# Product-key rankings at one step a slot, and a gather ring of ten rows from slot 80 on

## The chip, the cores and the metric

One NeuronCore of a Trainium2 chip runs one kernel launch. The metric is device time in microseconds. The engines are TensorE (PE; PEld is its weight load), VectorE (DVE), ScalarE (ACT), GpSimd (POOL, which here only issues gathers) and SyncE (SP, which issues plain loads). All are in order and meet by semaphores.

## What is computed

A decoder trunk of two layers over 256 tokens of width 1024, in float32. Layer 0 mixes tokens by differential attention, layer 1 by a gated short convolution. Behind each mixer stands an expert layer (PEER): 8 heads, and for each head the 16 best of 128 x 128 experts by product keys.

```python
q = (xt @ w_q).reshape(T, PEER_HEADS, 2, PEER_HALF)
s = jnp.einsum('thpd,hpkd->thpk', q, sub_keys)
s_top, i_top = lax.top_k(s, PEER_TOPK)
cand = s_top[:, :, 0, :, None] + s_top[:, :, 1, None, :]       # 16 x 16 sums a head
best, pos = lax.top_k(cand.reshape(T, PEER_HEADS, -1), PEER_TOPK)
idx = jnp.take_along_axis(cand_idx, pos, axis=-1)
gates = jax.nn.softmax(best, axis=-1)
# for a token c and its 8 x 16 experts:
act = jnp.einsum('chkd,cd->chk', u_tab[ib], xb)
act = jax.nn.gelu(act) * gb
out = jnp.einsum('chk,chkd->cd', act, v_tab[ib])
```

Every token reads 128 rows of u and 128 of v in each layer, rows of 1024 float32 each: that is most of what the kernel moves.

## The kernel before, in words

The 256 tokens are two blocks of 128 (one token a partition), and with the two layers there are four windows n = 0 to 3: layer n // 2, block n % 2. A window has 128 slots, one for each of a token's 128 experts; the main loop runs over 512 slots. In a slot

- POOL gathers 128 rows of 2048 float32 (u and v of one expert for each token, 1 MB) into one row of `ring` (L620). `ring` has RING = 8 rows. Gather s may start when the matmuls of slot s - 8 are done (`v_used`), and the head's `idx` must be there (`idx_ready`, once in 16 slots).
- DVE waits for the landing and makes the dot product of the u half with `xf` (L1215, `dot`).
- ACT makes gelu, weight and `diag`, the weight on a diagonal of 128 x 128 (L829, L831, L835, `weigh`).
- PE multiplies `diag` with the v half into `acc` (L555, `add_expert`), two slots behind, and counts up `v_used`.

All other work of a window is done beside the slots of the window before it. Each piece is a generator ("side") that yields the slot at which its next step is due, and `along` runs what is due behind each slot's own work, on each engine's own loop. The due slots stand in `AT`, relative to slot (n - 1) x 128, so window n's entries lie in the slots of window n - 1 (and run over into its own). For window 0, which the straight code in `front` prepares, some chunks come late: LATE_RANK_PROJECT for heads 2 to 7, LATE_IN_PROJECT for the attention input of block 1.

The pieces that matter here: `x` turns h of the new layer into xT, `in0` to `in5` are the mixer's input projections, `out0`, `out1` its output, `f` turns h again, `wq0` to `wq3` are the four query projections for experts (two heads each). A projection is 8 steps at 8 slots (`project`, L318). 13 slots behind its start DVE begins `ranked` (L1013 and on): a generator of 16 steps with 15 yields between them: MAX8, FIND_INDEX8, MATCH_REPLACE8 and again for the scores, the candidate sums, the same for the candidates, then one-hot product and sum for the index, and `idx_ready`. `paced(steps, at, per_slot)` spreads them, so far two a slot; ACT's exponential of the gates (`exponential_gates`) follows at step 8 and DVE's `gate_values` at 9. `finish` adds `acc` to h one slot into the next window, and PE waits for that (`acc_read`) before it overwrites `acc`; `scale_for_mixer` follows for the windows that have a successor to prepare.

SP loads weights (2 MB each) in a fixed order into the two places of `wring`, each when its former content was used. `vrows` (V of attention, 8 KB a partition) and `bias` (8 KB) are used by windows 0 and 1 alone. `rows1` holds query rows and some mixer rows. PSUM banks alternate in the pools pp, tt, ss, ff, in the order in which PE takes them.

Of the kernel before, what the change touches and what calls it, by code (L numbers as in the profile page):

```python
# [11 lines left out]
ACT = mybir.ActivationFunctionType  # L12
AX = mybir.AxisListType

P = 128
D = 1024
# [12 lines left out]
RING = 8  # L29
WINDOWS = DEPTH * (SEQ // P)  # L30
# [26 lines left out]
def steady_of(n):  # L57
# [11 lines left out]
         wq0=94, wq1=104, wq2=114, wq3=124),  # L69
    dict(x=3, in2=8, in4=16, in3=24, in5=32, in0=40, in1=48, z0=26, z1=42, turn_z0=27, turn_z1=43, turn_g0=49, turn_g1=57,  # L70
         conv0=30, conv1=46, times=59, out0=62, out1=70, h0=71, f0=72, h1=79, f1=80, scale=80,
         wq0=84, wq1=94, wq2=104, wq3=114),
# [3 lines left out]
LATE_RANK_PROJECT = {1: 0, 2: 25, 3: 41}  # L76
LATE_IN_PROJECT = {2: 9, 1: 17, 3: 33}

# [34 lines left out]
def build(nc, consts, x_rows, x_cols, bias_rows, ffn_rows, w_qkv, w_o, conv_w_in, conv_w_out, peer_w_q, peer_keys, peer_uv, out):  # L113
    with ExitStack() as ctx:
# [30 lines left out]
        vrows = sb("vrows", [P, 2, D])  # L145
        bias = sb("bias", [P, HEADS, SEQ])
        kT = sb("kT", [P, HEADS * SEQ + 16])
        qTa = sb("qTa", [P, HEADS, P])
        yT = qTa
        scratch = sb("scratch", [P, 2 * D])  # L150
# [34 lines left out]
        dots = sb("dots", [P, RING])  # L185
        gelu = sb("gelu", [P, RING])
        weight = sb("weight", [P, RING])
# [40 lines left out]
        uv_in = [sem(f"uv_in{i}") for i in range(RING)]  # L228
# [29 lines left out]
        def ring_at(s):  # L258
            return (s + 4) % RING

        def slot(s):

            return ring[:, ring_at(s), :], uv_in[ring_at(s)], 16 * (s // RING + 1)
# [35 lines left out]
        def _(pe):  # L299
# [222 lines left out]
            def gated_input(n):  # L522
# [4 lines left out]
                for i, c in enumerate((2, 4, 3, 5, 0, 1)):  # L527
# [3 lines left out]
                    yield from project(pp, n, "in", c, xT, at[f"in{c}"])  # L531
# [69 lines left out]
        def _(pool):  # L601
            for n in range(WINDOWS):
                for k in range(SLOTS):
# [3 lines left out]
                    if s < RING:  # L607
                        if ring_at(s) < 2:
                            written(pool, ff, (1, "in", 4))
                        elif ring_at(s) < 4:  # L610
                            written(pool, ff, (1, "in", 5))
                        elif ring_at(s) < 6:
# [11 lines left out]
        def _(act):  # L624
# [76 lines left out]
            def front():  # L701
# [28 lines left out]
                copy_y(0, 1)  # L730
                copy_f(0, 0)
# [12 lines left out]
            def rank(n, c, at, rank_at):  # L744
# [6 lines left out]
                yield rank_at + 8  # L751
# [50 lines left out]
            def gated_input(n):  # L802
                at = steady_of(n)
                for c in range(2):
                    yield at["x"] + c + 1
                    if c == 0:
                        written(act, pp, (n - 1, "wq", 3))
                    first = n // 2 * KT + 4 * c
                    copy_scaled((n, "x", c), xT[:, 4 * c:4 * c + 4, :], gain_mix[:, first:first + 4])
# [14 lines left out]
            def weigh(s):  # L824

                r = s % RING
                at = s % (2 * SLOTS)
                act.wait_ge(dot_done, s + 1)
                nc.scalar.activation(gelu[:, r:r + 1], dots[:, r:r + 1], ACT.Gelu_apprx_tanh).then_inc(gelu_done, 1)  # L829
# [446 lines left out]
```

## Time and profile before

| | us |
|---|---|
| three runs: median (lowest to highest) | 1601.99 (1601.55 to 1603.75) |
| the profiled execution | 1602.38 |
| its span | 1600.5 |
| PE busy | 1362.0 (85%) |
| DVE busy | 1012.6 (63%) |
| ACT busy | 593.4 (37%) |
| POOL busy | 559.7 (35%) |

The span runs from the first instruction to the last. The page of the profile cuts it into 40 slices of 40 us; for each it gives every engine's busy share in tenths and what the DMA engines moved in GB/s. A GB/s figure below its neighbours is transfer time lost. The list of waits says which engine waited for what, in total; the chain of waits goes back from the end by what released each step. Slots can be told in the trace by counting the dot products (L1215): slot 0 begins at 109.7 us, slot 128 at 498.2, slot 256 at 888.9, slot 384 at 1274.7.

### The profile page before, as it was taken

Reading aid. Unit: us, or ns where it says so; the run is one execution under the profiler, and the core shown is the slowest. Engines: PE = TensorE matmul, PEld = TensorE weight load, DVE = VectorE, ACT = ScalarE, POOL = GpSimd, SP = SyncE. Lnnn points to the kernel's source line nnn. Section 1 sums busy time; section 2 is a strip of 40 time slices with the busy share of each in tenths; the row PEclk is TensorE's granted clock in tenths of the full one; section 3 lists DMA queues with packets and bytes.
Section 4 is the critical chain, followed back from the end, with each engine's and each line's share of the span. In section 5 each row is a group of like instructions: output and inputs, shape, how many; then the busy total and the mean of one; then the engine's idle time right before and its main releaser. Section 6 shows DMA issues by size and latency. Waiting matters only on the chain.

```text
span 1600.5 us, 12987 instructions
## 1 busy us (share of the span) xinstructions
PE 1362.0 (85%) x3288; PEld 583.8 (36%) x3288; DVE 1012.6 (63%) x2442; ACT 593.4 (37%) x1809; POOL 559.7 (35%) x516
## 2 busy tenths in 40 slices
PE   7899899797987998897987799979888778777776
PEld 3454344343433343333433343434343332222222
DVE  4576879855498854445598854444568875444444
ACT  1324354533334442333334442333334443333333
POOL 0023333343333343352433343433333344333331
PEclk9999999899999999999999899999999999999999
DMA  9469999999999999999999899999999999999997
GB/s 399 197 245 422 422 413 414 368 395 421 422 425 414 400 424 421 422 422 422 422 422 422 349 398 423 422 422 422 422 425 418 351 347 423 421 421 422 421 422 321
DMA packets 82440, 639.67 MB, mean 400 GB/s; under 512 B 9152, under 2 KB 9280, under 8 KB 10560
## 3 DMA queue, kind: packets, MB, share of 16 engines
q0 software_dynamic: 73728, 536.90, 81.6%
q1 hardware_dynamic: 7344, 95.95, 14.3%
q10 hardware_dynamic: 1296, 6.00, 0.9%
q8 instruction: 28, 0.46, 0.1%
q14 instruction: 44, 0.36, 0.1%
HBM read 637.77 MB, written 1.05 MB: 399 GB/s over the span
## 4 chain that ended last, share of the span: by engine, by line
DMA 32%; DVE 29%; PE 29%; ACT 6%; issue 4%; DVEq 0%; POOL 0%; SPq 0%; POOLq 0%; ACTq 0%
DMA ring<-in_peer_uv_dram,idx 31%; PE acc L555 17%; DVE ring L1215 12%; PE pp L318 8%; DVE top_i L1001 2%; DVE pos L1001 2%; DVE top L997 1%; PE acc L318 1%; ACT L829 1%; DVE pick L1043 1%; DVE best L997 1%; DVE row_f L1046 1%; DVE pick L1040 1%; ACT weight L831 1%; ACT L699 1%
## 5 line engine op out<-in xcount | busy, mean ns | idle before, releaser
L555 PE MATMUL acc<-ring,diag 128*128 128x512 f32 x2048 | 1002.7, 617 | 169.4 <-ACT diag L835 155.7
L1215 DVE CUSTOM_DVE_ANT_0 ring<-ring,xf 128x1024 f32<-128x1024 f32 x512 | 624.8, 1226 | 486.9 <-DMA ring<-in_peer_uv_dram,idx 475.7
L620 POOL DMA_INDIRECT ring<-in_peer_uv_dram,idx x512 | 559.5, 1093 | 1017.2 <-PE acc L555 889.9
L555 PEld LDWEIGHTS acc<-ring,diag 128*128 128x128 f32 x2048 | 380.7, 195 | 720.9 <-issue 704.0
L829 ACT ACTIVATE gelu<-dots 128x1 f32<-128x1 f32 x512 | 103.5, 202 | 859.9 <-DVE dots L1215 859.5
L318 PE MATMUL pp<-wring,xT 128*128 128x512 f32 (+1 forms) x496 | 247.7, 590 | 1.2 <-ACT xT L639 1.2
L835 ACT ACTIVATE diag<-const,weight 128x128 f32<-128x128 f32 x512 | 205.4, 401 | 16.7
L831 ACT ACTIVATE weight<-gelu,gates 128x1 f32<-128x1 f32 x512 | 150.8, 295 | 16.6
L318 PEld LDWEIGHTS pp<-wring,xT 128*128 128x128 f32 x496 | 94.8, 194 | 109.9 <-issue 107.0
L318 PE MATMUL pp<-wring,qTa 128*128 128x512 f32 x112 | 57.2, 599 | 0.0
L331 PE MATMUL tt<-const,rows 128*128 128x128 f32 x144 | 23.8, 291 | 22.4 <-ACT rows L633 12.0
L1215 DVE DVE_READ_ACCUMULATOR2_ANT dots<- 128x1 f32 x512 | 42.3, 83 | 0.0
L390 PE MATMUL ss<-keysT,qT 128*128 128x128 f32 x128 | 20.7, 311 | 23.2 <-issue 23.2
L997 DVE MAX8 top<-score 128x8 f32<-128x128 f32 x128 | 28.1, 281 | 10.0 <-ACT score L695 9.3
L331 PEld LDWEIGHTS tt<-const,rows 128*128 128x128 f32 x144 | 17.4, 146 | 46.2 <-ACT rows L633 23.2
L1001 DVE FIND_INDEX8 top_i<-top,score 128x8 uint32<-128x128 f32 x128 | 34.2, 285 | 0.0
L318 PEld LDWEIGHTS pp<-wring,qTa 128*128 128x128 f32 x112 | 21.5, 193 | 26.8 <-issue 26.8
L390 PEld LDWEIGHTS ss<-keysT,qT 128*128 128x128 f32 x128 | 18.4, 217 | 35.2 <-issue 35.2
L1001 DVE FIND_INDEX8 pos<-best,pick 128x8 uint32<-128x256 f32 x64 | 26.1, 419 | 0.0
L318 PE MATMUL pp<-wring,xf 128*128 128x512 f32 x48 | 24.9, 601 | 0.0
L997 DVE MAX8 best<-pick 128x8 f32<-128x256 f32 x64 | 24.2, 417 | 0.6
L829 ACT ACT_TABLE_LOAD x19 | 24.4, 1283 | 0.3
(109 smaller groups left out, 570.2 us busy)
## 6 DMA issues: line engine op xcount, KB each, us to landing
wring<-in_peer_w_q_dram SPq DMA_DIRECT2D x16, 2048.0 KB, 11.7
wring<-in_conv_w_in_dram SPq DMA_DIRECT2D x12, 2048.0 KB, 11.7
wring<-in_w_qkv_dram SPq DMA_DIRECT2D x5, 2048.0 KB, 12.3
ring<-in_peer_uv_dram,idx POOLq DMA_INDIRECT x512, 15.3
wring<-in_conv_w_out_dram SPq DMA_DIRECT2D x4, 2048.0 KB, 11.8
ring<-in_w_qkv_dram SPq DMA_DIRECT2D x3, 2048.0 KB, 32.1
wring<-in_w_o_dram SPq DMA_DIRECT2D x3, 2048.0 KB, 12.7
ring<-in_w_qkv_dram SPq DMA_DIRECT2D x2, 1024.0 KB, 8.7
```

The lines of the kernel that those rows point to most:

```text
L318: mm = nc.tensor.matmul(bank[:, 0:width], src[:, k, :], by_row[:, k, columns], start=(k == 0), stop=(k == KT - 1))
L331: t = nc.tensor.transpose(bank[:, j * P:(j + 1) * P], tile, ident)
L390: mm = nc.tensor.matmul(bank[:, j * P:(j + 1) * P], qT[:, j, :], keysT[:, 4 * c + j, :], start=True, stop=True)
L555: mm = nc.tensor.matmul(acc[half][:, :], diag[:, s % RING, :], row[:, D + half * 512:D + (half + 1) * 512], start=(k == 0), stop=(k == SLO ...
L620: nc.gpsimd.indirect_dma_start(dst, None, uv_dram, bass.IndirectOffsetOnAxis(idx[:, at:at + 1], 0)).then_inc(landed, 16)
L699: nc.scalar.activation(best_e[:, js[0]:js[-1] + 1, :], best_e[:, js[0]:js[-1] + 1, :], ACT.Exp).then_inc(best_exp, len(js))
L829: nc.scalar.activation(gelu[:, r:r + 1], dots[:, r:r + 1], ACT.Gelu_apprx_tanh).then_inc(gelu_done, 1)
L831: nc.scalar.activation(weight[:, r:r + 1], gelu[:, r:r + 1], ACT.Copy, scale=gates[:, at:at + 1]).then_inc(weight_ready, 1)
L835: nc.scalar.activation(diag[:, r, :], ident, ACT.Copy, scale=weight[:, r:r + 1]).then_inc(diag_ready, 1)
L997: ins = nc.vector.max(t, v)
L1001: ins = nc.vector.max_index(i, t, v)
L1215: nc.vector.tensor_tensor_reduce(row[:, 0:D], row[:, 0:D], xf[:, s // SLOTS % 2, :], 1.0, 0.0, ALU.mult, ALU.add, dots[:, s % RING:s % RIN ...
```

## The change

`pieces(n, c)` gives the steps a slot of ranking (n, c): one, but two for the rankings (0,1), (0,2) and (1,0). The ACT and DVE steps for the gates move behind the longer ranking (`gates_from`). The wq projections get other due slots: 94, 104, 116, 128 for window 1, and 84, 98, 112, 126 for windows 2 and 3. Since the last one now overlaps `x` of the next window, `x` is turned into a tile of its own, `xTm`, the second half of `rows1`, and the queries take only the first half; ACT's waits follow.

`vrows` and `bias` become views of one tile, `spare`, 16 KB a partition, and from slot 80 on `spare` gives two more ring rows. Slots 80 and 81 are gathered into them once attention is done with bias and V (`logit_max` at 4, `values` (1,1) written); every later slot waits for the matmuls of ten slots before. `dots`, `gelu` and `weight` get 16 columns; `diag` stays at 8.

```diff
 RING = 8
+LONG_RING = 10
+LONG_FROM = 80
+SMALL = 16
...
-         wq0=94, wq1=104, wq2=114, wq3=124),
+         wq0=94, wq1=104, wq2=116, wq3=128),
...
-         wq0=84, wq1=94, wq2=104, wq3=114),
+         wq0=84, wq1=98, wq2=112, wq3=126),
...
+RANK_PIECES = {(0, 1): 2, (0, 2): 2, (0, 3): 1, (1, 0): 2}
...
+def pieces(n, c):
+
+    return RANK_PIECES.get((n, c), 1)
+
+
+def gates_from(n, c):
+
+    return 15 // pieces(n, c) + 1
...
-        vrows = sb("vrows", [P, 2, D])
-        bias = sb("bias", [P, HEADS, SEQ])
+        spare = sb("spare", [P, KT * CHUNK])
+        vrows = spare[:, 0:2 * D].rearrange("p (b d) -> p b d", b=2)
+        bias = spare[:, 2 * D:].rearrange("p (h k) -> p h k", h=HEADS)
...
+        xTm = rows1[:, D:2 * D].rearrange("p (k t) -> p k t", k=KT)
...
-        uv_in = [sem(f"uv_in{i}") for i in range(RING)]
+        uv_in = [sem(f"uv_in{i}") for i in range(LONG_RING)]
...
-        def ring_at(s):
-            return (s + 4) % RING
+        row_of = [(s + 4) % RING for s in range(RING)]
+        while len(row_of) < LONG_FROM:
+            row_of.append(row_of[-RING])
+        row_of += range(RING, LONG_RING)
+        while len(row_of) < ALL:
+            row_of.append(row_of[-LONG_RING])
+        row_uses = [row_of[:s].count(row_of[s]) for s in range(ALL)]
+        ring_rows = [ring[:, r, :] for r in range(RING)]
+        ring_rows += [spare[:, r * 2 * D:(r + 1) * 2 * D] for r in range(LONG_RING - RING)]
...
-            return ring[:, ring_at(s), :], uv_in[ring_at(s)], 16 * (s // RING + 1)
+            return ring_rows[row_of[s]], uv_in[row_of[s]], 16 * (row_uses[s] + 1)
...
-            return rows1[:, c * CHUNK:(c + 1) * CHUNK]
+            return rows1[:, c % 2 * CHUNK:(c % 2 + 1) * CHUNK]
...
-                    yield from project(pp, n, "in", c, xT, at[f"in{c}"])
+                    yield from project(pp, n, "in", c, xTm, at[f"in{c}"])
...
+                    elif s < LONG_FROM:
+                        pool.wait_ge(v_used, s - RING + 1)
+                    elif s < LONG_FROM + LONG_RING - RING:
+                        pool.wait_ge(logit_max, 4)
+                        written(pool, pp, (1, "values", 1))
                     else:
-                        pool.wait_ge(v_used, s - RING + 1)
+                        pool.wait_ge(v_used, s - LONG_RING + 1)
...
-                if n == 1 and c == 0:
-                    written(act, pp, (0, "wq", 3))
+                if n and c == 0:
+                    written(act, pp, (n - 1, "wq", 3))
...
+                written(act, pp, (0, "in", 5))
                 copy_f(0, 0)
...
-                yield rank_at + 8
+                yield rank_at + gates_from(n, c)
                 exponential_gates(n, c)
...
-                    if c == 0:
-                        written(act, pp, (n - 1, "wq", 3))
+                    if c == 0 and n == 3:
+                        written(act, pp, (2, "in", 1))
...
-                yield from paced(ranked(n, c), at, 2)
-                yield at + 9
+                yield from paced(ranked(n, c), at, pieces(n, c))
+                yield at + gates_from(n, c) + 1
                 gate_values(n, c)
```

## Rows read from the trace of the kernel before

**Rows 1.** The page: busy time; DMA share (tenths) and GB/s by slice.

```profile
PE 1362.0 (85%) x3288; PEld 583.8 (36%) x3288; DVE 1012.6 (63%) x2442; ACT 593.4 (37%) x1809; POOL 559.7 (35%) x516
...
DMA  9469999999999999999999899999999999999997
GB/s 399 197 245 422 422 413 414 368 395 421 422 425 414 400 424 421 422 422 422 422 422 422 349 398 423 422 422 422 422 425 418 351 347 423 421 421 422 421 422 321
DMA packets 82440, 639.67 MB, mean 400 GB/s; under 512 B 9152, under 2 KB 9280, under 8 KB 10560
```

**Rows 2.** List of waits, whole span: total us, times, longest.

```profile
POOL ring L620 <- PE acc L555: 889.9, 480, 8.8
...
DVE ring L1215 <- DMA ring<-in_peer_uv_dram,idx: 475.7, 316, 6.3
...
DVE best_s L1065 <- ACT best_e L699: 19.0, 16, 1.4
...
PE acc L555 <- DVEq L1209: 12.8, 3, 4.9
```

**Rows 3.** Stretches: busy us of PE, PEld, DVE, ACT, POOL; clock, DMA, GB/s.

```profile
220.00:260.00 40.00, 40.00 (x124) 19.85 (x122) 31.88 (x96) 12.34 (x36) 14.06 (x15) 1.00 1.00 404
280.00:340.00 60.00, 48.20 (x122) 21.56 (x121) 48.73 (x133) 30.86 (x91) 25.28 (x23) 0.91 0.94 367
480.00:540.00 60.00, 49.42 (x130) 22.42 (x129) 52.29 (x162) 26.69 (x74) 20.24 (x18) 0.94 0.99 402
600.00:860.00 260.00, 225.59 (x534) 98.58 (x533) 149.54 (x339) 91.66 (x285) 96.75 (x85) 0.96 1.01 422
880.00:960.00 80.00, 68.79 (x156) 29.89 (x155) 54.16 (x137) 34.08 (x101) 30.18 (x26) 0.91 0.94 374
960.00:1240.00 280.00, 245.83 (x583) 106.52 (x582) 157.79 (x338) 97.51 (x303) 100.79 (x93) 0.96 1.01 422
1240.00:1320.00 80.00, 61.46 (x139) 25.11 (x138) 66.80 (x185) 34.21 (x100) 32.69 (x29) 0.96 0.91 350
1320.00:1580.00 260.00, 204.92 (x422) 71.53 (x421) 128.28 (x209) 93.42 (x312) 103.86 (x105) 1.00 1.01 421
```

**Rows 4.** Chain of waits inside the plateau: start us, us, what.

```profile
1369.83 1.23 DVE ring L1215
...
1372.21 1.97 PE acc L555 x4
...
1374.44 15.25 DMA ring<-in_peer_uv_dram,idx
...
1389.71 1.23 DVE ring L1215
```

**Rows 5.** Gathers (L620) issued in 1240:1320 us, time from issue to landing.

```profile
DMA to landing us min/median/max: 5.2/7.8/12.5
```

**Rows 6.** Dots back to back: ns min/median/max, first and last start us.

```profile
L1215 DVE CUSTOM_DVE_ANT_0 ring<-ring,xf x6: 1221/1223/1225, 1303.6 to 1309.3; 128x1024 f32<-128x1024 f32 x6
```

**Rows 7.** Dot products during the ranking of slots 353 to 361.

```profile
L1215 DVE CUSTOM_DVE_ANT_0 ring<-ring,xf x9: 1224/1224/1226, 1178.3 to 1203.8; 128x1024 f32<-128x1024 f32 x9
```

**Rows 8.** Dot products over the next cycle of ten slots.

```profile
L1215 DVE CUSTOM_DVE_ANT_0 ring<-ring,xf x11: 1222/1226/1227, 1208.2 to 1239.4; 128x1024 f32<-128x1024 f32 x11
```

**Rows 9.** DVE by line and form in 1178.3:1205.4: busy us, mean ns, idle before.

```profile
L1043 DVE TENSOR_TENSOR pick<-pick,top_f 128x1024 f32<-128x1024 f32 x1 | 1.2, 1224 | 0.0
```

**Rows 10.** Timeline of DVE at slots 257 and 259: start us, us, what.

```profile
893.23 1.51 DVE L1207 TENSOR_TENSOR h<-h,acc 128x512 f32<-128x512 f32 x2
...
902.94 1.23 DVE L875 CUSTOM_DVE_ANT_0 scratch<-h 128x1024 f32<-128x1024 f32 x1
...
906.45 1.23 DVE L1215 CUSTOM_DVE_ANT_0 ring<-ring,xf 128x1024 f32<-128x1024 f32 x1 [0.19 <-DVE scale_mix L871]
```

**Rows 11.** By line, whole span: busy us, mean ns of one, idle before.

```profile
L318 PE MATMUL pp<-wring,xT 128*128 128x512 f32 (+1 forms) x496 | 247.7, 590 | 1.2 <-ACT xT L639 1.2
```

**Rows 12.** Weight loads (L583, SP), whole span, time from issue to landing.

```profile
DMA to landing us min/median/max: 7.8/11.8/25.5
```

More of the change, by code:

```diff
@@ L184, in build @@
         gains = sb("gains", [P, 2])
-        dots = sb("dots", [P, RING])
-        gelu = sb("gelu", [P, RING])
-        weight = sb("weight", [P, RING])
+        dots = sb("dots", [P, SMALL])
+        gelu = sb("gelu", [P, SMALL])
+        weight = sb("weight", [P, SMALL])
         diag = sb("diag", [P, RING, P])
@@ L607, in _ @@
                     if s < RING:
-                        if ring_at(s) < 2:
+                        if row_of[s] < 2:
                             written(pool, ff, (1, "in", 4))
-                        elif ring_at(s) < 4:
+                        elif row_of[s] < 4:
                             written(pool, ff, (1, "in", 5))
-                        elif ring_at(s) < 6:
+                        elif row_of[s] < 6:
                             written(pool, ff, (1, "in", 0))
@@ L805, in gated_input @@
                     yield at["x"] + c + 1
-                    if c == 0:
-                        written(act, pp, (n - 1, "wq", 3))
+                    if c == 0 and n == 3:
+                        written(act, pp, (2, "in", 1))
                     first = n // 2 * KT + 4 * c
-                    copy_scaled((n, "x", c), xT[:, 4 * c:4 * c + 4, :], gain_mix[:, first:first + 4])
+                    copy_scaled((n, "x", c), xTm[:, 4 * c:4 * c + 4, :], gain_mix[:, first:first + 4])
                 for c in (2, 4, 3, 5, 0, 1):
@@ L824, in weigh @@
             def weigh(s):
-                r = s % RING
+                r, m = s % RING, s % SMALL
                 at = s % (2 * SLOTS)
                 act.wait_ge(dot_done, s + 1)
-                nc.scalar.activation(gelu[:, r:r + 1], dots[:, r:r + 1], ACT.Gelu_apprx_tanh).then_inc(gelu_done, 1)
+                nc.scalar.activation(gelu[:, m:m + 1], dots[:, m:m + 1], ACT.Gelu_apprx_tanh).then_inc(gelu_done, 1)
                 act.wait_ge(gelu_done, s + 1)
-                nc.scalar.activation(weight[:, r:r + 1], gelu[:, r:r + 1], ACT.Copy, scale=gates[:, at:at + 1]).then_inc(weight_ready, 1)
+                nc.scalar.activation(weight[:, m:m + 1], gelu[:, m:m + 1], ACT.Copy, scale=gates[:, at:at + 1]).then_inc(weight_ready, 1)
                 act.wait_ge(weight_ready, s + 1)
@@ L834, in weigh @@
                     act.wait_ge(v_used, s - RING + 1)
-                nc.scalar.activation(diag[:, r, :], ident, ACT.Copy, scale=weight[:, r:r + 1]).then_inc(diag_ready, 1)
+                nc.scalar.activation(diag[:, r, :], ident, ACT.Copy, scale=weight[:, m:m + 1]).then_inc(diag_ready, 1)
             front()
@@ L1124, in late @@
                 yield at
-                yield from paced(ranked(0, c), at, 2)
-                yield at + 9
+                yield from paced(ranked(0, c), at, pieces(0, c))
+                yield at + gates_from(0, c) + 1
                 gate_values(0, c)
@@ L1158, in experts @@
                 yield at
-                yield from paced(ranked(n, c), at, 2)
-                yield at + 9
+                yield from paced(ranked(n, c), at, pieces(n, c))
+                yield at + gates_from(n, c) + 1
                 gate_values(n, c)
@@ L1215, in dot @@
                 nc.vector.tensor_tensor_reduce(row[:, 0:D], row[:, 0:D], xf[:, s // SLOTS % 2, :], 1.0, 0.0, ALU.mult, ALU.add,
-                                               dots[:, s % RING:s % RING + 1]).then_inc(dot_done, 1)
+                                               dots[:, s % SMALL:s % SMALL + 1]).then_inc(dot_done, 1)
             front()
```

## The prediction

> **What bounds the kernel now.** I began with the page [rows 1]. No engine is full: PE is busy for 85% of the span, DVE for 63%. The DMA line stands at 9 almost everywhere, and the GB/s line has a plateau at 421 to 425 with dents. Then the list of waits [rows 2]: POOL, which issues the gathers, waits 889.9 us for PE to release ring rows (acc), and DVE waits 475.7 us for gathers to land. So the gathers are a closed loop of 8 ring rows, and the transfer itself sets the pace where the loop is full. The table by stretch says where it is not [rows 3]: 422, 422 and 421 GB/s in the three long stretches, but 404, 367, 402, 374 and 350 GB/s in five short ones. At 422 GB/s as the full rate, the transfer time lost in a dent is its length times (422 minus rate)/422: 1.7 us in 220:260, 7.8 in 280:340, 2.8 in 480:540, 9.1 in 880:960 and 13.6 in 1240:1320. Together 35.0 us. What is left of the span is 639.67 MB at 422 GB/s (1516 us), the start before the gathers, and the drain behind the last one, none of which the change touches.
>
> What makes the dents? In all five DVE is busy for most of the time, 66.8 of 80 us in the last [rows 3]. The loop's own time in the plateau is in the chain of waits [rows 4]: from one dot product to the one eight slots later 19.88 us (2.485 a slot), of which 15.25 us is the gather from its issue on and 4.6 us dot, gelu, weight, diag, matmul and release. A gather with an empty queue before it lands in 5.2 us [rows 5]. So DVE may lag behind the landings by about 15.25 - 5.2 = 10 us before the queue runs dry. Where DVE is the bound, dots with nothing between them follow each other in (1309.3 - 1303.6)/5 = 1.14 us [rows 6], so 2.485 - 1.14 = 1.35 us a slot is free for side work. During a ranking 8 slots take 1203.8 - 1178.3 = 25.5 us [rows 7]: 25.5 - 8 x 1.14 = 16.4 us of ranking in 16 steps, two a slot, 2.05 us where 1.35 are free. Each ranking therefore adds 0.7 x 8 = 5.6 us of lag. With its gate step the cycle is 10 slots in 1239.4 - 1208.2 = 31.2 us against 24.9 us of transfers [rows 8], 6.3 us of lag each. Four of them in a row, less 5 us for a weight load (2.10 MB at 422 GB/s), give about 20 us of lag and lost transfer before slot 393: past the 10 us, and the dent is explained.
>
> **The change, part by part.**
> Rankings one step a slot. The same instructions, 16.4 us, over 16 slots: 1.02 us a step on average, and the largest single step is 1.22 us [rows 9]. All are under 1.35 us, so such a ranking adds no lag. The wq projections of windows 2 and 3 move to 84, 98, 112, 126, so a cycle is 14 slots: 34.8 us of transfer time against 14 x 1.14 + 16.4 + 0.6 (gates) = 33.0 us. The 1.4 us that DVE waits at worst for ACT's exponential [rows 2] arises when dots are back to back and fades when it waits for landings anyway; at its worst 34.4, still under 34.8.
> Stage around 384: four cycles over some 60 slots, 149 us of transfers. DVE: 68.4 of dots, 65.6 of rankings, 2.4 of gates, 1.5 for adding acc to h [rows 10]: 137.9. No lag beyond 4 us, so the 13.6 us go; I take 13.3.
> Around 256: the same plus the mixer's scale, 902.94 to 906.45 = 3.5 us [rows 10]: 141.4 against 149. Burst at slots 257 to 259: 5 us over two slots, lag 5 to 7 us. Of 9.1 us I take 8.8.
> Around 128: ranking (1,0) keeps two steps a slot, and (1,2) now begins at 129 while (1,1) runs to 132. Slots 129 to 132 hold 8 steps (8.2), a gate step (0.6) and 5.0 of adding and scale: 13.8 against 5.4 free, 8.4 us of lag on top of some 2. That is over the limit of 8 rows with its PE wait below and under that of ten. Of 2.8 us I take 2.6.
> Around slots 54 to 70 (280:340) only ranking (0,3) is spread; attention's steps stay, and eight rows stay. The bounds are 0 and 7.8 us; the ranking's 5.6 us of lag are the larger part of what fills the slack, so I take 5.0. 220:260 has ranking (0,2) as before: 0.
>
> A ring of ten from slot 80. Two more gathers in flight add 2 x 2.485 = 5.0 us of slack: 15 us. In the plateau this is worth nothing: the transfers are back to back and a gather only waits longer in the queue. It covers the bursts at 128 and 256, and the wait of PE for acc_read (12.8 us in three, the longest 4.9) [rows 2], which puts off the release of two rows. Slots 80 and 81 wait for logit_max and values (1,1), which PE issues at slot 64, while POOL comes to slot 80 after v_used 72: nothing waits. Behind them on POOL's in-order queue slot 82 waits for v_used 73 only. A slot now issues ten ahead, so slot 128 wants its idx when v_used is 119, against a ranking done at 115; 240 against 246 at the next boundary; later heads have 15 slots or more to spare. Cost 0.
>
> The moved projections. Each is 8 slots of two PE records of 0.5 us [rows 11] beside the 1.97 us of a slot's own matmuls [rows 4]: 23.8 us against 8 x 2.485 + 5.0 = 24.9 us with its weight load. The counts are unchanged and the wq ones lie further apart. ACT's copies and SP's loads keep their order: queries, turned and scores move with their chunk. The load of (n+1,in,4) waits for (n,wq,3) to be written, now at slot 133 or 135, and is wanted at 144: at least 8 slots, 20 us, against a median load of 11.8 us [rows 12]. Hidden; if the cover were gone it would be 11.8 us three times at most. x in its own tile (xTm) takes away ACT's wait for (n-1,wq,3) that would now bite; the waits added on (0,in,5) and (2,in,1) are for matmuls long done; dots, gelu, weight of 16 columns: 0.
>
> Sum: 13.3 + 8.8 + 2.6 + 5.0 = 29.7 us, and 1602.4 - 29.7 = 1572.7 in terms of the profiled execution (span 1600.5 plus 1.9 around it), which is 0.4 us above the median of the runs. I say 1572.5.
>
> A rule against it stands beside this sum. Rows 1 show 400 GB/s on average and rows 3 422. The Trainium skill (DMA: Bandwidth & Descriptors, Specifications) gives the HBM limit of a core as about 358 GB/s. By that the stream would be bound by HBM and the kernel would need some 1787 us for its bytes; the trace is faster than that, so the measurement decides.
>
> **Rivals.**
> B, only the deeper ring counts (8%): the lag comes not from the steps' density but from what holds PE at a boundary, its wait for acc_read. For it: PE's wait is real [rows 2]. Against it: the lag is there by slot 383 before any boundary work. It gives at most 5.0 us at each boundary: 2.8 + 5 + 5 = 12.8, hence 1589.6.
> C, the plateau rises (4%): deeper queue, higher rate. The rows' best stretch is 422 and the page's best slice 425 [rows 1, 3]: 0.7% of some 1200 us is 8 us more, 1564. Against it: the rate is 421 to 422 whether a gather spends 8 or 15 us in the queue. The Trainium skill (same page, Where 436 GB/s comes from) puts the fabric's ceiling at 435 GB/s; by that it could be an estimated 36 us, about 1537. No row comes near it.
> D, it does not do what it says (4%): rankings overlap, the lag is only moved, and the dents deepen at 128 as they vanish elsewhere: 1602.
> E, slower (4%): weight loads. Ten gathers queued ahead make each load later; PE waits in order, and behind the waiting projection stand all add_expert calls, hence v_used and every gather. The place is the eight tight loads a window (spacing 8 slots, 24.9 us with the load's own time). If a load took 30 us, 18 loads x 5.1 = 92 us, about 1665; it outweighs the gain from 26.6 us a load on. For it: the longest load in the trace took 25.5 us [rows 12]. Against: the median is 11.8 us beside eight queued gathers, and in proportion to ten that is 14.8.
>
> **How the numbers follow.** Forecast A: 80%, 1572.5, its own range 1565 to 1585: below, all 35.0 us and a little of C; above, nothing from 280:340 (5 us) and 2 to 3 us left in each boundary. The range of 8 in 10 is that one; B, D and E lie above it, C at its lower edge. About 0.2% (3 us) is what a measurement can tell from no change. Faster 0.92 (A, B, C), within 0.2% 0.04 (D), slower 0.04 (E).
>
> **What would show it.** In the profile after: GB/s at 421 or 422 in the slices of slots 256 and 384, no slice of the second half under 415 but the last; DVE's wait for landings spread over the rankings, where before it waited for none; gathers from slot 82 on landing about 5 us later after their issue in the plateau (20 us for 15.3); dots during rankings 2.5 us apart. A dent left at 280:340 of 2 to 3 us. The forecast is wrong if the dents stay with DVE idle in them (B), if PE waits for wring (E), or if DVE is still busy without a pause through slots 353 to 400 (D).

## The result, and the profile after

The changed kernel takes 1580.78 us (median of 4 runs, 1580.00 to 1582.67) beside 1601.77 us for the kernel before on the same chip: a ratio of 0.9872, 95% interval 0.9857 to 0.9887. It is faster by 21 us. The forecast was 1572.5, within 1565 to 1585: sign and mechanism were right, and of 29.7 us some 21 came. The profiled execution of after took 1580.29 us, its span 1578.5, 22.0 less than before.

The page of after, the lines that answer to [rows 1]:

```profile
PE 1358.9 (86%) x3288; PEld 588.6 (37%) x3288; DVE 1005.5 (64%) x2442; ACT 594.9 (38%) x1809; POOL 574.2 (36%) x516
...
DMA  9469999999999999999999999999999999999995
GB/s 399 206 245 422 422 409 409 406 422 422 422 422 421 423 423 421 423 423 421 422 422 421 407 424 422 423 422 421 423 421 422 421 407 421 421 421 422 421 422 241
DMA packets 82441, 639.68 MB, mean 405 GB/s; under 512 B 9152, under 2 KB 9280, under 8 KB 10560
```

The same engines do the same instructions. The dents of 347 to 400 GB/s of [rows 1] are shallow now (406 to 409), but the last slice is lower: 241 for 321.

The same five dents and three quiet stretches, by stretch, to set beside [rows 3] (columns as there; the last stretch ends at 1540 because the last gather now lands at 1570.1):

```profile
220.00:260.00 40.00, 39.57 (x122) 19.44 (x120) 32.57 (x98) 12.40 (x37) 14.61 (x14) 1.00 1.00 396
280.00:340.00 60.00, 50.26 (x129) 23.13 (x128) 51.30 (x138) 33.24 (x100) 30.63 (x25) 0.91 1.00 411
480.00:540.00 60.00, 50.90 (x128) 23.06 (x127) 51.22 (x149) 23.68 (x72) 20.72 (x18) 0.91 1.01 421
600.00:860.00 260.00, 224.43 (x529) 98.57 (x527) 143.46 (x315) 91.26 (x289) 100.39 (x89) 0.95 1.01 422
880.00:960.00 80.00, 74.31 (x179) 33.61 (x180) 62.01 (x164) 32.15 (x96) 29.97 (x26) 0.93 1.01 415
960.00:1240.00 280.00, 245.85 (x578) 107.93 (x577) 156.67 (x340) 101.38 (x318) 110.01 (x96) 0.95 1.01 422
1240.00:1320.00 80.00, 67.78 (x155) 27.25 (x154) 71.21 (x194) 35.58 (x103) 34.89 (x32) 0.98 1.01 414
1320.00:1540.00 220.00, 171.42 (x352) 59.40 (x350) 108.75 (x179) 81.79 (x267) 86.89 (x89) 1.00 1.01 421
```

What each dent lacks of 422 GB/s, by the forecast's formula: 2.5, 1.6, 0.1, 1.3 and 1.5 us, together 7.0 where before had 35.0. So 28 us of transfer time were closed, against 29.7 forecast. Yet the last gather landed only 22.0 us earlier, and 1.6 of them were there at the first gather, before anything differs. The missing part shows in the end of the stream, in stretches of 20 us. First after:

```profile
1520.00:1540.00 20.00, 15.64 (x32) 5.42 (x32) 9.87 (x16) 7.31 (x25) 7.55 (x9) 1.00 1.01 422
1540.00:1560.00 20.00, 15.63 (x32) 5.42 (x32) 9.87 (x16) 7.24 (x25) 4.62 (x5) 1.00 0.98 407
1560.00:1580.00 20.00, 11.73 (x24) 4.06 (x24) 7.54 (x12) 4.49 (x15) 0.00 (x0) 0.91 0.12 48
```

and the kernel before:

```profile
1560.00:1580.00 20.00, 15.75 (x34) 5.54 (x33) 9.31 (x17) 7.18 (x24) 6.55 (x7) 1.00 1.01 420
1580.00:1600.00 20.00, 12.56 (x26) 4.07 (x25) 8.43 (x14) 5.39 (x18) 0.00 (x0) 1.00 0.56 231
```

Before, the last gather landed at 1592.0 us; 231 x 20/422 = 10.9 us of transfers lie in the last 12.0 us, 1.1 us are lost. After, it landed at 1570.1; (407 + 48) x 20/422 = 21.6 us of transfers lie in the last 30.1, so 8.5 us are lost. (In both, 0.52 MB of output behind the last gather are counted, 1.2 us; the difference, 7.4 us, is the same without them.) PE still does 24 matmuls in the last stretch, four a slot, and the dots are still some 2.48 us apart, while next to nothing moves: 48 GB/s. Gathers complete one after another out of bytes that were nearly all moved before.

Why, the landing marks of the trace tell. Every gather leaves 16 marks on its row's semaphore. They are read here as one for each of the 16 DMA engines, made when its share is done; the trace doesn't name the engine, and the experiments below bear the reading out. The gather has landed with the last of the 16. From these marks (worked out from the trace's semaphore records: us from the first to the last of the 16, and in brackets from the last but one to the last):

```
slot    before      after        ring of 8   two steps a slot
128    3.3 (1.2)   2.6 (0.2)    2.7 (0.1)    3.3 (0.4)
272    0.5 (0.1)   6.7 (3.6)    2.1 (1.2)    4.3 (3.8)
392    1.8 (1.4)  11.8 (4.7)    5.5 (2.5)    3.7 (3.4)
511    2.7 (0.9)  10.8 (4.9)    6.6 (2.9)    2.6 (0.1)
```

The 16 engines drift apart. In after, at the end, 15 of them are at least 4.9 us ahead of the last one. Averaged over the 16 marks, the lead over the last one is 9.1 us at slot 511, and 1.7 us before: 7.4 us more, which is just what the drain lost more. Before, each dent let the slow ones catch up while the fast ones stood idle (0.5 us between first and last at slot 272, 1.8 at 392), and a mean over 16 engines counts that idling as loss even where the slowest engine doesn't pause. That is theory S below: the pace is that of the slowest DMA engine, so closing a dent gives only what the slowest engine idled. Its rival M: transfer time is what the mean rate says, and the rest was lost elsewhere.

### The profile page after: what moved, and what is told of

Its sections match the earlier page's. It is cut to its first block, busy times and chain, and to the rows that moved or that the text cites. A ratio compares the mean times of both kernels' runs of the same rounds, so it can differ in the third digit from the quotient of the medians.

```text
span 1578.5 us, 13059 instructions
## 1 busy us (share of the span) xinstructions
PE 1358.9 (86%) x3288; PEld 588.6 (37%) x3288; DVE 1005.5 (64%) x2442; ACT 594.9 (38%) x1809; POOL 574.2 (36%) x516
## 3 DMA queue, kind: packets, MB, share of 16 engines
q1 hardware_dynamic: 7344, 95.95, 14.5%
## 4 chain that ended last, share of the span: by engine, by line
DMA 43%; PE 32%; DVE 16%; issue 4%; ACT 4%; DVEq 0%; POOL 0%; SPq 0%; POOLq 0%; ACTq 0%
DMA ring<-in_peer_uv_dram,idx 24%; PE acc L578 19%; DMA spare<-in_peer_uv_dram,idx 18%; PE pp L341 9%; DVE ring L1244 5%; DVE spare L1244 1%; PE acc L341 1%; PE tt L354 1%; DVE top_i L1030 1%; ACT diag L864 1%; DVE row_f L1075 1%; DVE top L1026 1%; ACT weight L860 1%; DVE pick L1072 1%; DVE pick L1069 1%
## 5 line engine op out<-in xcount | busy, mean ns | idle before, releaser
L578 PE MATMUL acc<-ring,diag 128*128 128x512 f32 x1696 | 831.4, 619 | 126.9 <-ACT diag L864 117.1
L648 POOL DMA_INDIRECT ring<-in_peer_uv_dram,idx x424 | 476.9, 1125 | 832.2 <-PE acc L578 707.5
L1244 DVE CUSTOM_DVE_ANT_0 ring<-ring,xf 128x1024 f32<-128x1024 f32 x424 | 518.7, 1226 | 397.6 <-DMA ring<-in_peer_uv_dram,idx 387.4
L578 PEld LDWEIGHTS acc<-ring,diag 128*128 128x128 f32 x1696 | 318.1, 196 | 575.4 <-issue 562.7
L578 PE MATMUL acc<-spare,diag 128*128 128x512 f32 x352 | 172.9, 618 | 28.8 <-ACT diag L864 28.7
L1244 DVE CUSTOM_DVE_ANT_0 spare<-spare,xf 128x1024 f32<-128x1024 f32 x88 | 107.8, 1225 | 96.6 <-DMA spare<-in_peer_uv_dram,idx 95.2
L341 PE MATMUL pp<-wring,xT 128*128 128x512 f32 (+1 forms) x304 | 148.6, 585 | 1.2 <-ACT xT L667 1.2
L648 POOL DMA_INDIRECT spare<-in_peer_uv_dram,idx x88 | 97.1, 1104 | 144.1 <-PE acc L578 141.7
L578 PEld LDWEIGHTS acc<-spare,diag 128*128 128x128 f32 x352 | 65.2, 196 | 124.0 <-issue 123.8
L341 PE MATMUL pp<-wring,rows 128*128 128x512 f32 x192 | 98.8, 596 | 0.0
## 6 DMA issues: line engine op xcount, KB each, us to landing
wring<-in_peer_w_q_dram SPq DMA_DIRECT2D x16, 2048.0 KB, 11.9
wring<-in_conv_w_in_dram SPq DMA_DIRECT2D x12, 2048.0 KB, 11.9
wring<-in_conv_w_out_dram SPq DMA_DIRECT2D x4, 2048.0 KB, 11.9
```

The source lines that it names most:

```text
L341: mm = nc.tensor.matmul(bank[:, 0:width], src[:, k, :], by_row[:, k, columns], start=(k == 0), stop=(k == KT - 1))
L578: mm = nc.tensor.matmul(acc[half][:, :], diag[:, s % RING, :], row[:, D + half * 512:D + (half + 1) * 512], start=(k == 0), stop=(k == SLO ...
L648: nc.gpsimd.indirect_dma_start(dst, None, uv_dram, bass.IndirectOffsetOnAxis(idx[:, at:at + 1], 0)).then_inc(landed, 16)
L1244: nc.vector.tensor_tensor_reduce(row[:, 0:D], row[:, 0:D], xf[:, s // SLOTS % 2, :], 1.0, 0.0, ALU.mult, ALU.add, dots[:, s % SMALL:s % SM ...
```

## The experiments

The diffs are against the changed kernel, with cuts marked by dots. Ratios are to the kernel before, run beside each experiment.

**Which half of the change does it?** The ring of ten is taken back, the spread rankings stay:

```diff
-LONG_RING = 10
+LONG_RING = 8
```

> The changed kernel with a ring of eight throughout (LONG_RING = 8): the spread rankings alone. Theory S (the density of the rankings made the dents, and what is left is set by the slowest of the 16 DMA engines): most of the gain stays, about 1583 to 1588, with some us lost where adding acc to h and the mixer's scale meet a ranking at slots 128 and 256. Rival B (only the two extra rows count): the dents are back at 880:960 and 1240:1320 and the time is 1595 or more. If the two parts share the gain evenly: about 1590.

Measured: 1581.04 us (1580.53 to 1582.33), ratio 0.9861 (0.9844 to 0.9877). That is less than all three expectations, and it can't be told from the whole change (0.9872; a repetition of the changed kernel gave 1580.37, 0.9856, 0.9838 to 0.9875). By stretch:

```profile
480.00:540.00 60.00, 50.04 (x124) 22.63 (x123) 49.38 (x143) 23.54 (x70) 18.77 (x17) 0.91 0.99 399
...
880.00:960.00 80.00, 73.20 (x178) 33.05 (x179) 61.94 (x166) 31.52 (x96) 27.27 (x26) 0.93 1.00 410
...
1240.00:1320.00 80.00, 67.79 (x155) 27.27 (x154) 70.95 (x190) 35.22 (x102) 35.55 (x32) 0.98 1.01 410
```

Its dents at 480:540 (399), 880:960 and 1240:1320 are deeper than those of after (421, 415, 414): 3.1, 0.9 and 0.8 us more by the mean rate, and yet the end isn't later. The engines' spread at the end is 6.6 us for 10.8. Under M after should have been 5 us faster; under S the two rows only let fast engines run further ahead. Their mean lead at slot 511 is 5.2 us here and 9.1 in after.

The other half alone: the ring of ten, with all rankings at two steps a slot at their old slots:

```diff
-         wq0=94, wq1=104, wq2=116, wq3=128),
+         wq0=94, wq1=104, wq2=114, wq3=124),
...
-         wq0=84, wq1=98, wq2=112, wq3=126),
+         wq0=84, wq1=94, wq2=104, wq3=114),
...
-RANK_PIECES = {(0, 1): 2, (0, 2): 2, (0, 3): 1, (1, 0): 2}
+RANK_PIECES = {}
...
-    return RANK_PIECES.get((n, c), 1)
+    return RANK_PIECES.get((n, c), 2)
```

> The changed kernel with all rankings at two steps a slot and the old due slots of the query projections: the ring of ten alone. Theory S: the 7 us at slots 64 to 80 are lost again (eight rows there), the lag of slots 353 to 393 still exceeds the slack by some 5 us, so 1590 to 1594. Rival B: 1580 to 1584, since the ring alone covers the lag.

Measured: 1592.77 us, ratio 0.9934 (0.9917 to 0.9950), 10.7 us faster than before.

```profile
280.00:340.00 60.00, 48.29 (x122) 21.73 (x121) 48.98 (x133) 30.88 (x91) 27.19 (x24) 0.91 0.95 365
480.00:540.00 60.00, 49.96 (x129) 23.13 (x128) 52.22 (x162) 26.70 (x74) 19.68 (x18) 0.91 1.01 422
...
880.00:960.00 80.00, 67.02 (x150) 28.21 (x149) 56.48 (x140) 35.27 (x107) 32.36 (x27) 0.94 0.97 387
...
1240.00:1320.00 80.00, 60.76 (x139) 24.78 (x138) 67.17 (x178) 35.63 (x105) 36.65 (x29) 0.96 0.95 369
```

Ten rows add slack at three boundaries, as rival B had it: by the mean rate 2.8 + 2.5 + 3.6 = 8.9 us. Here deep dents remain, the engines are level at the end (spread 2.6 us), and the credit is full. The halves are not additive: alone they give 22 and 11 us, together 21 to 22. What the ring covers, the spread rankings no longer need.

A ring of nine (LONG_RING = 9), between the two:

> The changed kernel with a ring of nine from slot 80. Theory S: the fast DMA engines run ahead one gather less, which costs nothing while the slowest one always has work: within 2 us of 1580.8. If each row of the ring buys 2.5 us at each of the stages that still drain it: 1583 to 1588. It is also the control of the run with the extra loads, which needs the freed memory.

Measured: 1581.49 us (1579.57 to 1581.62), ratio 0.9865 (0.9848 to 0.9881). Eight, nine and ten rows are one time; the spread at the end is 6.6, 8.9 and 10.8 us.

**Which stage gives how much?** Only ranking (0,3) spread, ring of eight, the rest as before (`RANK_PIECES = {(0, 3): 1}`, default 2, the old wq slots):

> Ring of eight, every ranking at two steps a slot and at the old due slots, but (0,3) spread over 16 slots. It should give what the stage at slots 64 to 80 gives by itself, 7 us: 1594 to 1596. If spreading works only where all rankings are spread: no gain.

Measured: 1595.9 us, ratio 0.9968 (0.9958 to 0.9978): 5.1 us, where the expectation counted 7, and 280:340 is at 410 GB/s for 367. The term for slots 54 to 70 stood at 5.0. (The 7 us were read from two traces and held the 1.6 us that after was ahead at slot 0.)

Only the four rankings of window 3, slots 353 to 400 (ring of eight, every other ranking at two steps a slot and at its old due slots):

```diff
...
-AT = AT + (AT[2],)
+AT = AT + (dict(AT[2], wq0=84, wq1=98, wq2=112, wq3=126),)
...
-RANK_PIECES = {(0, 1): 2, (0, 2): 2, (0, 3): 1, (1, 0): 2}
+RANK_PIECES = {(3, 0): 1, (3, 1): 1, (3, 2): 1, (3, 3): 1}
```

> Ring of eight, only the four rankings of window 3 spread (with their new due slots). The stage around slot 384 alone. Theory S: 9 us, as between slots 384 and 400 of the two traces, 1592 to 1594. By the mean rate, as forecast: 13 us, 1588 to 1590.

Measured: 1590.33 us, ratio 0.9933 (0.9916 to 0.9949), 10.7 us. Its trace:

```profile
1240.00:1320.00 80.00, 68.84 (x172) 29.13 (x171) 70.72 (x199) 36.94 (x106) 39.19 (x33) 1.00 1.01 421
```

The dent is closed entirely, 13.5 us by the mean rate (350 to 421), and 10.7 arrive: between the two expectations. At slot 272 this kernel's engines stood level (0.4 us, dents before it are intact); at its end they are 7.6 us apart. The mean lead at slot 511 is 5.0 us for 1.7 before, 3.3 more, about the 2.8 us that are missing. The interval of 2.6 us either way wouldn't tell S from M by the time alone; the run with load on a single engine, below, does.

**Is it PE's instruction packets that hold one engine back?** The page lists packets of kind instruction (q8: 28 of 16 KB, q14: 45 of 8 KB) on the same DMA engines. PE's are taken down by doing the upper half of acc in the first slot of each window only; this kernel leaves out the expert sum of columns 512 to 1023 but for that slot:

```diff
-                for half in range(2):
+                for half in range(2 if k == 0 else 1):
...
-                                          start=(k == 0), stop=(k == SLOTS - 1))
+                                          start=(k == 0), stop=(half == 1 or k == SLOTS - 1))
```

> The changed kernel without three quarters of nothing but PE's second matmul of a slot: the upper 512 columns of the expert sum are made from the first slot of each window alone, the rest is left out. Gathers, dots, loads and all waits stay. PE's instruction stream becomes shorter (some 1000 of its 6600 instructions and their weight loads go), and with it the 16 KB packets in which it is fetched, from 28 to about 20. Theory S (one DMA engine carries them, 1.07 us each, and it sets the pace): about 8 us less, 1572 to 1575. Rival M (the mean rate): 0.13 MB less is 0.3 us, so 1580 to 1581. The landings' spread at the end falls from 10.8 us to 5 or less by S.

Measured: 1579.66 us, ratio 0.9864 (0.9847 to 0.9880). The expectation of 1572 to 1575 fell. q8 went from 28 to 20 packets and PE's matmuls from 3288 to 2272, and the engines' spread at the end stayed (11.1 us for 10.8); the last engine is 7.2 us behind the last but one, for 4.9. PE's packets don't sit on the slow engine. A third of PE's matmuls are gone, and the time is that of the changed kernel. Two dents did close, from 396 and 411 GB/s:

```profile
220.00:260.00 40.00, 29.95 (x89) 14.09 (x87) 35.69 (x111) 14.55 (x40) 15.27 (x14) 0.93 1.01 422
280.00:340.00 60.00, 39.33 (x91) 16.87 (x92) 48.10 (x124) 30.01 (x93) 29.46 (x25) 0.81 1.01 421
```

By the mean rate that is 3.9 us, and the measured 1.1 us isn't told from nothing.

**Does load on a single engine cost time while the mean rate doesn't change?** To the ring of nine, SP adds 72 loads of one partition, 8 KB each (three behind every weight load of windows 2 and 3, each waiting for the one before it):

```diff
+                if n > 1:
+                    for _ in range(3):
+                        ...
+                        sp.dma_start(spare[0:1, 2 * D:4 * D], in_dram[1][0][0:1, 0:2 * D]).then_inc(extra_in, 16)
+                        extras += 1
```

> As the ring of nine, with 72 extra loads of one row of 8 KB, three behind each weight load of windows 2 and 3. Together 0.59 MB, which is 1.4 us at 422 GB/s if all 16 DMA engines share one pace. Theory S: one row goes through one DMA engine, 72 x 0.31 = 22 us of its time. If that is the engine that lags already, the kernel becomes some 22 us longer; if it is another one, that engine first uses up its lead of about 10 us and the kernel becomes about 10 us longer. Rival M (the mean rate bounds, the missing 8 us lie elsewhere): 1 to 2 us longer.

Measured: 1588.0 us (1585.81 to 1590.90), ratio 0.9907 (0.9887 to 0.9926), 6.5 us over the ring of nine that ran beside it. The added bytes are 0.59 MB, 1.4 us at 422 GB/s. The stretch that holds part of the extra loads, here and in the ring of nine:

```profile
960.00:1240.00 280.00, 240.69 (x550) 104.26 (x551) 152.23 (x329) 98.74 (x309) 95.32 (x91) 0.94 1.00 412
...
960.00:1240.00 280.00, 243.24 (x575) 105.48 (x574) 157.27 (x339) 100.50 (x317) 106.92 (x96) 0.96 1.01 422
```

412 GB/s for 422, with more bytes to move: the others wait for the one. 72 packets of 309 ns are 22.2 us on that engine; 6.5 came out, less than either of S's expectations (10 and 22). The other 15.7 us fell into time that this engine had to spare, by S; the trace can't show that, since it doesn't name the engine. M's 1 to 2 us are excluded. That SP sent its weight loads late isn't the cause: they land in 11.9 us for 11.8, and no row of waits has PE waiting for wring.

**A load cut for 15 engines.** If the slow engine could be spared, the others would set the pace. Seven weight loads were cut into 120 and 8 partitions:

```diff
+                    sp.dma_start(place[0:120, :], matrix[c][0:120, :]).then_inc(landed, 16)
+                    sp.dma_start(place[120:P, :], matrix[c][120:P, :]).then_inc(w_rest_in, 16)
```

> The changed kernel with seven of its 2 MB weight loads cut in two: 120 partitions, and 8 partitions. If a load of 120 partitions is spread over 15 of the 16 DMA engines and the rest over 8 of the 15, the sixteenth has 7 x 128 KB = 34 us less to move. Theory S, if that engine is the lagging one: 8 to 10 us less, 1571 to 1573, and the landings' spread goes to about 3 us. If the lagging one is among the 8 that take the rest: 3 to 4 us more, 1584 to 1585. If it is another: 1581. Rival M: 1581 in each case, since the bytes are the same.

Measured: 1646.56 us, ratio 1.0275 (1.0255 to 1.0296): 66 us slower than the changed kernel, 9.4 us for each cut load, and outside every expectation. The spread of the 16 marks jumps to 15 to 29 us around them. Queue q1 here, and in after:

```profile
q1 hardware_dynamic: 7393, 95.95, 15.8%
...
q1 hardware_dynamic: 7344, 95.95, 14.5%
```

The same 95.95 MB take 15.8% of the engines' time, though the span is longer, with 49 packets more. It settles nothing about S; why the cut costs so much was not followed up.

**Whose instruction packets are they, then?** In the quiet end of after, two landings come late by 1.0 us. The timeline of DVE there (start us, us, what, in brackets its idle time before):

```profile
1327.14 1.23 DVE L1244 CUSTOM_DVE_ANT_0 ring<-ring,xf 128x1024 f32<-128x1024 f32 x1 [1.13 <-DMA ring<-in_peer_uv_dram,idx]
...
1330.64 1.23 DVE L1244 CUSTOM_DVE_ANT_0 ring<-ring,xf 128x1024 f32<-128x1024 f32 x1 [2.27 <-DMA ring<-in_peer_uv_dram,idx]
...
1333.08 1.23 DVE L1244 CUSTOM_DVE_ANT_0 ring<-ring,xf 128x1024 f32<-128x1024 f32 x1 [1.21 <-DMA ring<-in_peer_uv_dram,idx]
```

From dot to dot 3.50 us, then 2.44 where 2.485 is the pace. The same stands at 1483.14, 61 slots later. Each time one 8 KB packet of queue q14 was taken just before (1329.1 and 1480.8 us), and the gather's packet beside it took 958 and 968 ns for the usual 312. Two more packets of q14, at 1395.3 and 1474.9, stand beside gather packets of 687 ns, and no landing is late there. In the 61 slots between the two late landings DVE has 121 instructions in the trace, two a slot, the reading of the accumulator among them. So theory S2: the slowest engine is the one that also fetches DVE's instructions, and each fetch costs it about 1 us. The test is to add instructions on an engine with time to spare: five tiny ones behind each of 213 quiet slots, on DVE:

```diff
+                if s in QUIET:
+                    for j in range(5):
+                        at = s % 12 * 5 + j
+                        nc.vector.memset(small[:, at:at + 1], 0.0)
```

> The changed kernel with five tiny DVE memsets behind each dot of 213 slots in which DVE has no side work. DVE's time for them (at most 0.6 us a slot) lies in its wait for the landing. Theory S2 (the lagging DMA engine is the one that fetches DVE's instructions, 8 KB or some 128 instructions a time, about 1 us of delay each): 1065 instructions are 8.3 fetches, 8 us longer than the changed kernel, 1588 to 1590. Rival M (the mean rate of the 16 engines bounds): 0.07 MB, 0.2 us, no change. Rival D (DVE's own time matters): the GB/s would fall in the slots with memsets and the chain would pass through DVE.

Measured: 1588.97 us (1586.90 to 1590.05), ratio 0.9909 (0.9892 to 0.9926); the changed kernel itself again, beside it 1580.37. So 8.6 us more. The trace:

```profile
960.00:1240.00 280.00, 245.13 (x566) 106.18 (x565) 158.26 (x634) 100.60 (x314) 100.82 (x95) 0.95 1.01 419
...
1320.00:1540.00 220.00, 169.81 (x348) 59.04 (x348) 113.11 (x597) 80.16 (x262) 86.45 (x88) 1.00 1.01 419
...
q14 instruction: 53, 0.43, 0.1%
```

DVE is busy 113.11 of 220 us in the last stretch, half idle, so its work isn't what costs. In all of slots 412 to 504 the dot starts within 0.02 us of its landing. Eight packets more (53 for 45; 1065 instructions, 133 a packet) and 8.6 us: 1.07 us each. From slot 401 on, after has two landings that are late by 1.0 us; this run has six, 18 or 19 slots apart in its quiet slots, which at seven DVE instructions a slot is again one in 126 to 133. The run with load on a single engine has none there. The last engine is now 12.1 us behind the last but one (4.9 in after).

The same 1065 instructions on ACT:

```diff
+                        nc.scalar.activation(small[:, at:at + 1], ident[:, 0:1], ACT.Copy)
```

> The mirror of the run before: the same number of tiny ACT instructions in the same slots. S2: ACT's instructions are fetched by another DMA engine, which has a lead of about 10 us over the slowest; 8.3 fetches use it up at most: within 1 us of the changed kernel. If the lag comes from any instruction fetch alike: 8 us longer, as with DVE. M: no change.

Measured: 1581.65 us (1580.19 to 1582.98), ratio 0.9861 (0.9842 to 0.9880), 1.3 us over its neighbour, where S2 allowed 1 and a lag from any fetch would have been 8. Also 53 packets of q14, but the engine that carries ACT's had time to give: the lead of the last but one at the end fell from 4.9 us (5.9 in the neighbour) to 1.5. It is the engine, and not the number of packets or instructions, that decides.

The changed kernel again, as their neighbour:

> The changed kernel as it is, beside the two that follow, so that effects of a few us can be told on the same chip. 1580 to 1582 by every theory.

Measured: 1580.37 us (1579.75 to 1580.82).

**The other way: fewer instructions on DVE.** In the changed kernel DVE waits for its own former step behind each of its steps. Here it waits only when the next one is to be issued, which is often a slot later, and the reciprocal root takes two Newton steps for three:

```diff
-                dve.wait_ge(dve_step, done[0])
...
+            def settle():
+                if waited[0] < done[0]:
+                    waited[0] = done[0]
+                    dve.wait_ge(dve_step, done[0])
...
-                for _ in range(3):
+                for _ in range(2):
```

> The changed kernel with a shorter instruction stream for DVE: the wait for a side step's own result is put ahead of the next side instruction instead of behind the step, so that a dot no longer carries two waits (about 200 separate semaphore instructions go), and the inverse roots take two Newton steps instead of three (52 instructions). S2: some 250 instructions are two fetches of 8 KB, 2 us less, 1578 to 1579, which five rounds can hardly tell. A gain of 5 us or more would mean that the separate semaphore instructions cost more than their fetch. Rival M: no change.

Measured: 1573.39 us (1573.08 to 1575.37), ratio 0.9818 (0.9805 to 0.9832): 7 us faster than the changed kernel (1580.37, on another chip; the kernel before took 1602.8 on both), and the fastest of all. But not by S2: q14 has 43 packets for 45, worth 2 us. Where the 7 us lie shows in the stretch of the first gathers, 80 to 120 us; first after, then this kernel:

```profile
80.00:120.00 40.00, 37.28 (x118) 20.19 (x117) 32.03 (x115) 11.68 (x31) 9.93 (x9) 1.00 0.69 259
```

```profile
80.00:120.00 40.00, 37.28 (x115) 19.92 (x114) 34.69 (x116) 11.34 (x30) 10.55 (x10) 1.00 0.79 304
```

(304 - 259) x 40/422 = 4.3 us of transfers more. Its waits say the same: POOL's one wait for the first ranking is 97.6 us,

```profile
POOL ring L648 <- DVEq L897: 97.6, 1, 97.6
```

for 101.8 in after. The first gather lands at 103.7 us, in the other traces at 106.9 to 109.8. From slot 80 on the gain is nearly constant: its dot starts 5.8 us earlier than in after, that of slot 511 6.7 us. So before the first gather and in the attention stages DVE's chain is on the path, and shortening it pays there at once; the rest of the kernel, at the pace of the slow engine, gave 0.9 us for two packets fewer. Which of the two edits gave how much wasn't separated. The expectation's size failed because it priced the fetches alone.

## Why the prediction was right, and where its size was wrong

**Spread rankings add no lag: held.** DVE's timeline of after in window 3, with steps of a ranking behind its dots (the lines of single steps are left out but two):

```profile
1181.56 1.22 DVE L1244 CUSTOM_DVE_ANT_0 ring<-ring,xf 128x1024 f32<-128x1024 f32 x1 [0.44 <-DMA ring<-in_peer_uv_dram,idx]
1182.71 0.08 DVE L1244 DVE_READ_ACCUMULATOR2_ANT dots<- 128x1 f32 x1
1182.71 0.75 DVE L1026 MAX8 best<-pick 128x8 f32<-128x256 f32 x2
1184.04 1.23 DVE L1244 CUSTOM_DVE_ANT_0 spare<-spare,xf 128x1024 f32<-128x1024 f32 x1 [0.57 <-DMA spare<-in_peer_uv_dram,idx]
...
1186.53 1.22 DVE L1244 CUSTOM_DVE_ANT_0 spare<-spare,xf 128x1024 f32<-128x1024 f32 x1 [0.45 <-DMA spare<-in_peer_uv_dram,idx]
...
1189.01 1.23 DVE L1244 CUSTOM_DVE_ANT_0 ring<-ring,xf 128x1024 f32<-128x1024 f32 x1 [0.46 <-DMA ring<-in_peer_uv_dram,idx]
```

The dots are 2.48 to 2.49 us apart, the pace of the transfers, and each waits about half a us for its gather: 2.5 was the forecast. In [rows 7] the dots of a ranking waited for nothing and stood 3.19 us apart. At the end of the four rankings the dot of slot 383 comes 1.7 us after its landing; before it came 10.9 us after, past the 10 us of slack that the forecast had. The largest lag of slots 353 to 400 is 3.9 us for 15.3, and the forecast allowed 4.

**Stages.** The landing of the same slot, before and after, tells what each stage gave (the mean-rate column is before's loss less after's, from [rows 3] and the table above):

```
up to the end of   landed earlier by   stage gave   mean rate closed   forecast
slot 0                 1.6 us             1.6             -                -
slot 80                7.1                5.5        -0.8 + 6.2          5.0
slot 160               7.2                0.1            2.7             2.6
slot 272              11.4                4.2            7.8             8.8
slot 400              21.1                9.7           12.1            13.3
slot 511              22.0                0.9             -                -
```

The 1.6 us of slot 0 are there before anything changed and are scatter of one execution. The term of slots 54 to 70 was 5.0, and 5.5 came (5.1 in the run with that ranking alone). From landing 0 to landing 80 the traces with ranking (0,3) at two steps a slot take 239.8 to 240.5 us, and those with it spread 233.0 to 235.0. From slot 80 on the three terms 2.6, 8.8 and 13.3 stood at 24.7; the mean rate rose as if 22.6 were gained, and landings moved by 14.8 with the quiet end. **The step that failed** is the first formula: that a dent costs its length times (422 minus rate)/422 on the path. It is right while the engines are level, as in the kernel before up to slot 80 and in the ring of ten alone. It overstates by what the fast engines idle while the slow one still works, and so does the sentence ahead of the prediction that a GB/s figure below its neighbours is transfer time lost. The 7.8 us that are missing after slot 80 stand again at the end of the stream (8.5 - 1.1 = 7.4 us more lost in the drain), where nothing comes after to use the lead. The prediction had called the drain untouched.

**Signs and readings that were off.** The prediction wanted no slice of the second half under 415 GB/s but the last. Two of the page stand at 407, behind slots 256 and 384, though DVE doesn't lag past its slack there; what keeps them wasn't followed up. The dent left at 280:340 is 1.6 us, where 2 to 3 were named. The moved projections were priced with PE records of 0.5 us where [rows 11] has 590 ns; with that the 23.8 us become 25.2, over the 24.9 of the cycle, so the sum didn't show by itself that they fit. The rate was said to be 421 to 422 whether a gather spends 8 or 15 us in the queue, but the 7.8 us of [rows 5] stand in the stretch of 350 GB/s; that a longer queue doesn't raise the rate is shown only by after.

**The ring of ten: no cost, as said; no gain either.** In the plateau the chain of after is

```profile
1367.88 1.23 DVE spare L1244
...
1370.26 1.97 PE acc L578 x4
...
1372.48 20.23 DMA spare<-in_peer_uv_dram,idx
1392.71 0.03 issue
1392.74 1.23 DVE spare L1244
```

20.23 us from issue to landing, where [rows 4] had 15.25 and the forecast 20; ten slots take 24.86 us, 2.486 each, as before. The bursts at 128 did come (dots of slots 132 to 140 trail their landings by 7 to 9 us, 8.4 on top of some 2 were forecast), and the ring covered them in the mean rate; but the 2.6 us booked for that were worth nothing at the end. Rival B's mechanism is real (the ring alone gives 11 us), but it is not what the change lives on.

**What was costed at nothing** held. The waits of after, to set beside [rows 2]:

```profile
POOL ring L648 <- PE acc L578: 707.5, 394, 10.3
...
DVE ring L1244 <- DMA ring<-in_peer_uv_dram,idx: 387.4, 277, 7.4
...
POOL spare L648 <- PE acc L578: 141.7, 84, 6.7
...
DVE spare L1244 <- DMA spare<-in_peer_uv_dram,idx: 95.2, 66, 6.6
...
PE acc L578 <- DVEq L1238: 9.6, 3, 3.6
...
DVE best_s L1094 <- ACT best_e L727: 7.9, 13, 1.4
```

DVE waits 387.4 + 95.2 = 482.6 us for landings, as before (475.7). No row has PE waiting for wring. The wait for ACT's exponential fell from 19.0 to 7.9 us. Weight loads land 11.9 us after their issue, 11.8 before, with ten gathers queued for eight: rival E had nothing to work with. Rival C fell: the plateau stands at 421 and 422. The trace is above the limit of about 358 GB/s that the Trainium skill gives for a core (DMA: Bandwidth & Descriptors, Specifications), and 3% under the 435 GB/s that the same table gives as the fabric's ceiling: 422 is what this stream has.

## What to carry over

A dent in the mean rate of 16 DMA engines tells at most (within a us or two here) what can be won by closing it, and all of it only when the engines are level; look at how far the single landing marks of a transfer lie apart, and at how fast the stream ends. Side work on an engine that feeds a queue of transfers belongs spread to under the free time of each period (here 1.35 us a slot); that alone took 22 us, and more buffers added nothing to it. Then look for stretches with another bound: here the front, where DVE's own chain was worth another 7 us.

## What the runs showed of the hardware that was not expected

- The 16 DMA engines don't stay level under a full stream: 10.8 us between the first and the last mark of a gather after some 1300 us at 422 GB/s, 2.7 us where deep dents leave time to catch up.
- Instruction fetches share the DMA engines with data. On the engine of DVE's stream eight fetches of 8 KB cost 8.6 us, on that of ACT's 1.3 us, where there was slack. In after that explains landings late by 1.0 us behind the packets of 1329.1 and 1480.8 us; whether fetches make up all of the 10.8 us isn't shown.
- A gather has 128 packets of 8 KB, 8 for each of 16 engines if they share alike; at 309 to 312 ns they take 2.47 to 2.50 us, which is the plateau's 2.485 us a slot.
- 72 loads of one partition (8 KB) cost 6.5 us beside a stream that needs 1.4 us for their bytes.
- A 2 MB load cut into 120 and 8 partitions cost 9.4 us each beside the gathers. The cause is open.
